# Experts in plain fp32 on column tiles of the array, with a longer ring of weights

## What is computed

```python
def swiglu(h, w_gu, w_down):
    gt, up = jnp.split(h @ w_gu, 2, axis=-1)
    return (jax.nn.silu(gt) * up) @ w_down

def moe(h, w_r, b_r, w_gu, w_down):
    t = h.reshape(-1, shp[-1])
    logits = (t @ w_r).astype(jnp.float32) + b_r.astype(jnp.float32)
    top_v, top_i = lax.top_k(logits, TOP_K)
    wts = jax.nn.softmax(top_v, axis=-1)
    comb = jnp.sum(jax.nn.one_hot(top_i, N_EXPERTS) * wts[..., None], axis=1)
    out = jnp.zeros_like(t)
    for e in range(N_EXPERTS):
        out = out + comb[:, e:e + 1] * swiglu(t, w_gu[e], w_down[e])
```

## Time and profile before

| | |
|---|---|
| median of three runs | 1997.94 us (1997.94 to 1998.37) |
| span of the profiled execution | 1993.6 us |
| PE busy | 1947.5 us, 98% |
| DVE busy | 1556.5 us, 78% |
| ACT busy | 1135.9 us, 57% |
| DMA | 523.97 MB, 262 GB/s read and written over the span |
| mean granted TensorE clock | 0.987 |

### The profile page before, as it was taken

The page is one execution under the profiler, slowest core; times in us unless marked ns, Lnnn a source line. Parts: engine busy times, 40 slices in busy tenths (PEclk is TensorE's granted clock), DMA queues, the critical chain, the costliest instruction groups (busy, mean ns, idle before and its releaser), DMA issues.

```text
span 1993.6 us, 31431 instructions
## 1 busy us (share of the span) xinstructions
PE 1947.5 (98%) x11926; PEld 1657.1 (83%) x11926; DVE 1556.5 (78%) x2210; ACT 1135.9 (57%) x1385; POOL 240.4 (12%) x279
## 2 busy tenths in 40 slices
PE   7999999999999999999999999999999999999997
PEld 3778999899998788999788888888888888888886
DVE  6895448655673976377898989989889899898996
ACT  2214334545432233334677777777778777787774
POOL 2540432000005331340000000000000000000000
PEclk9999999999999999999999999999999999999999
DMA  9575444555551564435599999999999999899993
GB/s 348 183 289 202 147 149 176 200 181 185 176 175 64 201 218 138 169 108 198 187 362 365 353 338 339 360 365 351 343 330 364 368 350 343 330 361 369 342 357 126
DMA packets 143054, 523.97 MB, mean 263 GB/s; under 512 B 16192, under 2 KB 16704, under 8 KB 142272
## 3 DMA queue, kind: packets, MB, share of 16 engines
q1 hardware_dynamic: 140544, 508.82, 70.3%
q10 hardware_dynamic: 1728, 7.90, 1.2%
q0 software_dynamic: 640, 5.35, 0.7%
HBM read 515.57 MB, written 6.43 MB: 262 GB/s over the span
## 4 chain that ended last, share of the span: by engine, by line
PE 87%; DVE 7%; ACT 2%; POOL 2%; issue 1%; DMA 1%; ACTq 0%; DVEq 0%
PE bank L1041 28%; PE bank L1066 14%; PE bank L878 12%; PE bank L291 9%; PE bank L616 8%; PE bank L479 4%; DVE wlo L2414 3%; PE bank L495 2%; PE bank L966 2%; PE bank L1028 1%; ACT whi L1408 1%; PE bank L444 1%; PE bank L837 1%; PE bank L706 1%; DMA masks<-in_masks 1%
## 5 line engine op out<-in xcount | busy, mean ns | idle before, releaser
L2414 DVE TENSOR_TENSOR wlo<-ring,whi 128x1024 fp32r<-128x1024 f32 x756 | 910.0, 1221 | 145.2 <-ACT whi L1408 142.9
L1408 ACT ACTIVATE whi<-ring 128x1024 fp32r<-128x1024 f32 x756 | 799.5, 1060 | 293.9 <-PE bank L1041 146.1
L1041 PE MATMUL bank<-whi,gh 128*128 128x512 f32 x896 | 285.6, 400 | 2.1 <-DVE wlo L2414 0.9
L1041 PE MATMUL bank<-whi,gl 128*128 128x512 f32 x896 | 279.7, 393 | 0.0
L1041 PE MATMUL bank<-wlo,gh 128*128 128x512 f32 x896 | 278.9, 393 | 0.0
L291 PE MATMUL bank<-hT,ring 128*128 128x264 f32 x864 | 204.8, 397 | 5.7 <-issue 3.0
L291 PEld LDWEIGHTS bank<-hT,ring 128*128 128x128 f32 x864 | 166.1, 195 | 41.5 <-issue 11.4
L1041 PEld LDWEIGHTS bank<-wlo,gh 128*128 128x128 f32 x896 | 168.2, 188 | 39.0
L1041 PEld LDWEIGHTS bank<-whi,gl 128*128 128x128 f32 x896 | 168.1, 188 | 38.1
L1041 PEld LDWEIGHTS bank<-whi,gh 128*128 128x128 f32 x896 | 159.5, 188 | 32.3 <-DVE wlo L2414 3.2
L1066 PE MATMUL bank<-whi,eh 128*128 128x512 f32 x448 | 142.5, 399 | 0.3
(11 more groups left out here) (431 smaller groups left out, 3115.5 us busy)
## 6 DMA issues: line engine op xcount, KB each, us to landing
ring<-in_w SPq DMA_DIRECT2D x964, 512.0 KB, 5.2
out_gdns<-arena POOLq DMA_DIRECT2D x2, 2048.0 KB, 9.4
arena<-in_gdn ACTq DMA_DIRECT2D x2, 1536.0 KB, 7.1
xT<-in_x ACTq DMA_DIRECT2D x1, 1056.0 KB, 9.2
out_y<-hT SPq DMA_DIRECT2D x4, 264.0 KB, 2.1
arena<-in_gdn ACTq DMA_DIRECT2D x2, 512.0 KB, 3.8
masks<-in_masks ACTq DMA_DIRECT2D x1, 512.0 KB, 11.3
cpk<-in_cpk SPq DMA_DIRECT2D x1, 512.0 KB, 5.3
```

The source lines that it names most:

```text
L1041: ins = pe.matmul(o[half], x[:, k, mine], w[part][:, CH * half:CH * half + CH], start=k == 0 and n == 0, stop=k == KD - 1 and n == 2)
L1408: act.activation(whi[:, m % SPL, :], ring[:, r, :], ACT.Copy).then_inc(sem("hi_done"), 1)
L2414: v.tensor_tensor(wlo[:, m % SPL, :], ring[:, (low.base + m) % RING, :], whi[:, m % SPL, :].bitcast(F32), ALU.subtract).then_inc(sem("lo_d ...
```

## The change

Tokens and weights change places in the experts, and the split goes.

- The weights of an expert are now the stationary operand, in blocks of 128 x 128 like those of the other parts of the kernel (`_slots`, `_pairs`, `_blocks` in the layout). Each block is loaded in four tiles of 32 columns (`product`, `CT`), each with its own quarter of the output partitions, and `CAP` = 96 columns of tokens stream. The products are plain fp32, so there is no split of weights, tokens or hidden values: `high` and `low` are not called for experts, `gl`, `eh`, `el` and DVE's `gathered` are gone, `gh` becomes `gx` and the hidden values `ea`.
- Results come out features by tokens. Hidden values need no transposes. The down result does: ACT copies pairs of feature tiles to `ys`, and `turn` transposes them into banks 4 and 5, where `rows` reads them.
- The ring has twelve places for experts (`ERING`): the seven of `ring`, and five in `ring2` over the former split buffers. PE waits for the landing itself (`place_sem`), and `e_used`, counted by PE, frees a place for SP. The first twelve slots are loaded without a wait for PE.
- Silu and product go over four feature tiles at once (`BAT`). `ROWS`, `COMBINE` and `DCT` move by a slot. Two pairs of input loads share a semaphore. POOL clears `yh` and `yl` too, since `rows` now writes 96 of their 128 partitions.

The diff, cut to what the steps below speak of:

```diff
-CAP = 128
+CAP = 96
...
-NCH = FF // CH
+BAT = 4
+NCH = FT // BAT
+ERING = 12
+CT = P // 32
...
-        gh, gl = over("gh", [P, KD, PAIR], where(hT), 0), over("gl", [P, KD, PAIR], arena_at, 0)
-        eh, el = over("eh", [P, FT, CAP], arena_at, 2 * B1), over("el", [P, FT, CAP], arena_at, 2 * B1 + FT * CAP)
-        at_e = 2 * B1 + 2 * FT * CAP
-        erow = ar(at_e, 2, CH)
-        srow = ar(at_e + 2 * CH, 2, CH)
+        gx = over("gx", [P, KD, PAIR], where(hT), 0, F32)
+        ea = ar(2 * B1, FT, CAP)
+        at_e = 2 * B1 + FT * CAP
+        srow = ar(at_e, 2, BAT, CAP)
+        ys = ar(at_e + 2 * BAT * CAP, KD, CAP)
+        ring2 = over("ring2", [P, ERING - RING, SLOT * P], where(whi), 0, F32)
...
-        def silu_after(m):
-
-            return [c for c in range(NCH) if m == KD * (c + 1) + SPL - 1]
-
-        def turned_after(m):
-            return [c for c in range(NCH) if m == KD * (c + 1) + TURN + SPL]
+        def batch_after(m):
+
+            return [c for c in range(NCH) if m == 2 * BAT * (c + 1)]
+
+        def half_down_after(m):
+
+            return [p for p in range(KD // YP) if m == UP_S + FT * YP // SLOT * (p + 1)]
+
+        def place(m):
+
+            p = m % ERING
+            return ring[:, (MIX1_END + p) % RING, :] if p < RING else ring2[:, p - RING, :]
+
+        def place_sem(m):
+            p = m % ERING
+            return landed[(MIX1_END + p) % RING] if p < RING else landed2[p - RING]
+
+        def place_count(q, m):
+
+            p = m % ERING
...
+                def turn(self, q, p):
+
+                    pe.wait_ge(sem("e_ys"), q * (KD // YP) + p + 1)
+                    for m in range(YP * p, YP * p + YP):
+                        ins = pe.transpose(bank[4 + m // 4][0:CAP, P * (m % 4):P * (m % 4) + P], ys[:, m, :], ident)
+                    if YP * (p + 1) % 4 == 0:
+                        ins.then_inc(sem("ye_full"), 1)
...
+                def emptied(c):
+                    if a is not None or q or c >= 2:
+                        pe.wait_ge(sem("act_done"), q * NCH + (FT + 1 + max(c - 1, 0)))
+
+                def product(out, w, b, x, first, last):
+                    for j in range(CT):
+                        ins = pe.matmul(out[32 * j:32 * j + 32, :], w[:, b * P + 32 * j:b * P + 32 * j + 32], x,
+                                        start=first, stop=last)
+                    return ins
+
                 if sub == 0:
-                    pe.wait_ge(sem("gh_done"), pg * 4 + 4)
-                    pe.wait_ge(sem("gl_done"), pg * 4 + 4)
...
-                    c, k = s // KD, s % KD
-                    pe.wait_ge(sem("lo_done"), q * FFN_S + (base + s + 1))
-                    if k == 0 and c >= 2:
-                        pe.wait_ge(sem("act_done"), q * NCH + (FT + 1 + c - 1))
-                    w = [t[:, s % SPL, :] for t in (whi, wlo)]
-                    o = [bank[2 * (c % 2) + half][0:CAP, :] for half in range(2)]
-                    for n, (x, part) in enumerate(((gh, 0), (gh, 1), (gl, 0))):
-                        for half in range(2):
-                            ins = pe.matmul(o[half], x[:, k, mine], w[part][:, CH * half:CH * half + CH],
-                                            start=k == 0 and n == 0, stop=k == KD - 1 and n == 2)
-                            if n == 0 and half == 0:
-                                ins.then_inc(sem("spl_used"), 1)
-                    if k == KD - 1:
-                        ins.then_inc(sem("up_full"), 1)
-                    if k == TURN and c:
-                        turn(c - 1)
+                    f, half = s // 2, s % 2
+                    c = f // BAT
+                    pe.wait_ge(place_sem(s), place_count(q, s))
+                    if s % (2 * BAT) == 0:
+                        emptied(c)
+                    o = bank[2 * (c % 2) + half][:, CAP * (f % BAT):CAP * (f % BAT) + CAP]
+                    for k in range(KD):
+                        ins = product(o, place(s), k, gx[:, k, mine], k == 0, k == KD - 1)
+                    ins.then_inc(sem("e_used"), 1)
+                    if a is None and s == BACK and not (q == 0):
+                        self.turn(q - 1, KD // YP - 1)
                     if s in COMBINE:
                         self.combine(s - COMBINE[0], g)
...
-                for s in range(DOWN_S):
-                    m = UP_S + s
-                    pe.wait_ge(sem("lo_done"), q * FFN_S + (base + m + 1))
-                    if s % (CH // P) == 0:
-                        pe.wait_ge(sem("turned_done"), q * NCH + (s // (CH // P) + 1))
-                    w = [t[:, m % SPL, :] for t in (whi, wlo)]
-                    for n, (x, part) in enumerate(((eh, 0), (eh, 1), (el, 0))):
-                        for half in range(2):
-                            ins = pe.matmul(bank[6 + half][0:CAP, :], x[:, s, :], w[part][:, CH * half:CH * half + CH],
-                                            start=s == 0 and n == 0, stop=s == FT - 1 and n == 2)
-                            if n == 0 and half == 0:
-                                ins.then_inc(sem("spl_used"), 1)
-                            if s == FT - 1 and n == 2:
-                                ins.then_inc(sem("ye_full"), 1)
-                    if s == TURN:
-                        turn(NCH - 1)
-                    if sub and UP_S + s in GATHER:
-                        self.gather(GATHER.index(UP_S + s), pg + 1)
+                for m in range(KD):
+                    if m % YP == 0 and (a is not None or q or m > YP):
+                        pe.wait_ge(sem("e_ys"), q * (KD // YP) + (m // YP - 1))
+                    for k in range(FT):
+                        b = m * FT + k
+                        s, i = UP_S + b // SLOT, b % SLOT
+                        if i == 0:
+                            pe.wait_ge(place_sem(s), place_count(q, s))
+                        if m == 0 and k % BAT == 0:
+                            pe.wait_ge(sem("act_done"), q * NCH + (FT + 1 + k // BAT + 1))
+                        ins = product(bank[6 + m // YP % 2][:, CAP * (m % YP):CAP * (m % YP) + CAP], place(s), i, ea[:, k, :],
+                                      k == 0, k == FT - 1)
+                        if i == SLOT - 1:
+                            ins.then_inc(sem("e_used"), 1)
+                            for p in half_down_after(s - BACK):
+                                if p == 0:
+                                    pe.wait_ge(sem("dcT_done"), q * 1 + 1)
+                                self.turn(q, p)
+                            if sub and s in GATHER:
+                                self.gather(GATHER.index(s), pg + 1)
+                if a is not None:
+                    self.turn(q, KD // YP - 1)
...
-                    sp.wait_ge(sem("lo_done"), q * FFN_S + (FFN_S + s - RING + 1))
-                    r = (MIX1_END + s) % RING
-                    sp.dma_start(ring[:, r, :], w_in[e * FFN_S + (MIX1_END + s)]).then_inc(landed[r], 16)
+                    if not (s0 and s < ERING):
+                        sp.wait_ge(sem("e_used"), q * FFN_S + (s - ERING + 1))
+                    sp.dma_start(place(s), w_in[e * FFN_S + (MIX1_END + s)]).then_inc(place_sem(s), 16)
...
-                if k >= KD - LAG:
-                    s = k - (KD - LAG)
-                    n = MIX1_END + s
-                    high(n % RING, 16 * (n // RING + 1), s, FFN_S + s + 1)
...
+                for m in range(FFN_S + 1):
+                    for c in batch_after(m):
+                        act.wait_ge(sem("e_used"), q * FFN_S + m)
+                        if not (a is None and q == 0 and c < 2):
+                            act.wait_ge(sem("act_done"), q * NCH + (FT + 1 + c - 1))
+                        act.activation(srow[:, c % 2, :, :], four(bank[2 * (c % 2)]), ACT.Silu).then_inc(sem("silu_done"), 1)
+                    for p in half_down_after(m):
+                        act.wait_ge(sem("e_used"), q * FFN_S + m)
+                        act.activation(ys[:, YP * p:YP * p + YP, :],
+                                       bank[6 + p % 2][:, 0:YP * CAP].rearrange("p (a b) -> p a b", b=CAP), ACT.Copy).then_inc(sem("e_ys"), 1)
                     if m == ROWS:
...
-                    if l and m >= KD - LAG:
-                        low(m - (KD - LAG), FFN_S + m - (KD - LAG) + 1)
...
-                    if not (a is None and e == 0 and m < LAG):
-                        low(m, q * FFN_S + (FFN_S + m + 1))
-                    for c in silu_after(m):
+                    for c in batch_after(m):
                         v.wait_ge(sem("silu_done"), q * NCH + (FT + c + 1))
-                        v.tensor_tensor(erow[0:CAP, c % 2, :], srow[0:CAP, c % 2, :], bank[2 * (c % 2) + 1][0:CAP, :],
+                        v.tensor_tensor(ea[:, BAT * c:BAT * c + BAT, :], srow[:, c % 2, :, :], four(bank[2 * (c % 2) + 1]),
                                         ALU.mult).then_inc(sem("act_done"), 1)
```

(44 more changed lines are left out.)

90 lines of the change are left out of this document (35 added, 55 removed).

## The result

The changed kernel takes 2458.4 us (median of 4 runs) beside 1998.2 us for the kernel before: a ratio of 1.228, 95% interval 1.225 to 1.231. It is slower by 23%, where 1991 us was forecast. The span of the profiled execution is 2458.3 us.

The account below looks back on a forecast made before the run. PE paced the kernel before, DMA close behind; after, one DMA engine: 1.276 us data plus 0.24 code, 1.516 a slot over 659 slots from 963.7 to 1962.7. Span 1987.0, median 1991 us, 0.3% faster; range 1840 to 2055.

Parts of the forecast that it names:

- The reading of the kernel before: Expert stage: PE sets the pace at 1.50 us a slot, DMA is near its limit, ACT and DVE splits are hidden.
- PE's cost of a slot: Experts: 32 products of 21.7 ns, 0.69 us; PE's whole work falls from 1.50 to some 0.81 us a slot.
- The price of the code: Expert stage: PE's instruction packets, one every four slots at 0.95 us, add 0.24 us a slot on one DMA engine.
- DMA's cost of data: Expert weights: 524288 bytes a slot at the full-queue rate of 411 GB/s, 1.276 us; dearer bounds 1.372 and 1.421.
- rival 2: Expert weights arrive at the expert stage's slower rate: 1.612 to 1.661 us a slot, 2054 to 2087 us; chance 0.17.
- What moves around it: Before and beside the experts: root 2.7 us sooner, last token copy 0.45 for 0.60 us, first product at 959.7 for 962.54.
- The last residual: Norm before the experts: without DVE's subtraction at 926.70 it starts about 1.1 us sooner.
- the root's input: Norm before the experts: starts about 2.7 us sooner without DVE's subtractions; 0 if the root finds another wait.
- Rival 1: Expert stage: instructions cost nothing on the path, 1.291 us a slot, 1843 us; chance 0.27.
- Rival 3: Expert stage: PE's clock falls to 1.2 GHz while waiting, about 1.62 us a slot, 2060 us at most; 0.06 with others.
- the signs named: Expert windows, if right: PE waits for landings, SP for PE, about 230 q8 packets, near 345 GB/s, landing near 18 us.

Follow-up runs that it names:

- the two-tile kernel: The changed kernel with two weight tiles of 64 columns for each 128-column block in place of four of 32: 1996.9 us, ratio 0.9996 to the kernel before.
- the fastest: The two-tile kernel with its combine and gather steps issued in pairs: 1987.8 us, ratio 0.994 to the kernel before.
- the loops: The changed kernel plus extra fp32 products in hardware loops at PE's program end; 64 calls 8 times, 256 and 512 calls 4 times: 23.1, 45.6, 128.3 us.

## Why the prediction was wrong

**The reading of the kernel before** held: PE set its pace, and ACT's and DVE's splits lay hidden.

**PE's cost of a slot is the step that failed.** The duration was right: 21.7 ns a product by interpolation, 20.5 measured. The count was not. The 64 products of line 461 in the earlier trace rows are records; the code has 32 calls there for each layer (2 halves x 2 x 2 x 4). A plain fp32 call is two loads and two products in the records. So 32 calls a slot are 64 products, 1.31 us in place of 0.69, and 128 instructions in place of 64. The row that would have told it, x64 beside 32 calls, stood in the prediction's own evidence.

**The price of the code was read rightly and put in the wrong place.** 16.4 KB a packet, about 256 instructions, about 1 us on the queue: all as measured (1.09 us on average). But the forecast charged that microsecond to a DMA engine and asked what it does to the weights. What matters is the way from one block to the next as PE sees it: 1.1 to 1.7 us until the packet starts, 1.0 for the packet, 1.4 until PE goes on. PE has its products to cover that and nothing else. At 2.63 us of products to 3.7 us of way, it can't. The term was 0.24 us a slot; the stand is 2.19 - 1.31 = 0.88 with the other products.

The two errors belong together. With 64 instructions a slot, as counted, the code would have come at 64/256 x 4.28 = 1.07 us a slot, below the 1.28 of the weights, and by this reckoning the stand would have cost next to nothing (the two-tile kernel has 64 instructions a slot, and 37 us of code stands). The doubled count makes it 2.14, which decides. The corrected sum: 964.3 (first product) + 672 x 2.19 = 2436 us; the last products of line 1053 end at 2433.6, and the kernel 25 us later (23 in the kernel before).

**DMA's cost of data** (1.276 us a slot, 411 GB/s) was not tested, since no run here let the weights set the pace: the fastest brought 356 GB/s with PE busy for 97%. It stays open, and with it rival 2.

**What moves around it** was small, as said, and came out in sum but not in its parts. The forecast had the first product 2.8 us sooner. Counted from the start of the mixer's last product (926.34 before, 931.35 after), it comes after 33.0 us in place of 36.2, and after 32.9 to 33.5 in the other runs with this code. The last residual starts 1.2 us sooner by that count, as read (1.1), but the root's input (931.62 before) 1.3 us sooner and not 2.7. It finds another wait, as the low bound of that term allowed, for PE's products of the norm:

```profile
931.35 0.28 PE L641 MATMUL bank<-ml,ghi 128*128 128x264 f32 x1
931.67 0.17 DVE L2216 TENSOR_TENSOR tmp<-bank,mods 128x8 f32<-128x8 f32 x1 [1.99 <-PE bank L641]
935.30 0.43 DVE L1559 TENSOR_SCALAR tmp<-bank 128x264 f32<-128x264 f32 x1 [2.54 <-PE bank L428]
```

The other 1.9 us lie between there and the first product, where 0.15 was forecast. In that stretch the granted clock was first 0.50, the level of 1.2 GHz, for 6.8 us in place of 10.2, and the router's 48 products took 6.59 us in place of 7.51; why is open. That the sum came out was luck. (The first product came at 964.32 and not 959.7, since the mixer ended later; its last product started between 924.6 and 934.3 us in the runs with this code.)

**The rivals.** None gave the time. Rival 1, code that costs nothing, is the opposite of what happened. The Trainium skill, "Runtime: NRT & Kernel Launch", Instruction fetch mechanics, calls the crossing of a 16 KiB block mostly hidden; the trace agrees on the block (a stand every 256 instructions) and not on the hiding (363.5 us of stands from 1000 to 2400 us). The same section of the Trainium skill gives TensorE room for 2048 instructions; the loops don't contradict it, with a body of 1024 that stayed and one of 2048, beside the loop's own instructions, that was fetched anew. Rival 3 is out with a granted clock of 0.96. Of the signs named, the one that was decisive did its work: q8 packets were to be about 230 and are 395, and PE was to wait for landings and does not.

## What to carry to other kernels

Count instructions in the records, not calls in the source, before a price is put on them, and hold the time that 256 of them keep the engine against the time until the next code is there: here 3.7 to 4.4 us, so products of 20 ns written out run at 0.6 to 0.7 of their speed, while the same products in a loop of up to 1024 instructions run at full. Halving the calls with tiles of 64 columns, which cost the same for a block, took back the whole loss. Keep products of one tile size together: a change between 32 and 64 columns costs about 0.14 us.

## What the runs showed of the hardware

- A plain fp32 call is recorded as two loads and two products; a 128x128 block against 96 columns costs 2 x 111.9 = 224 ns in one tile, 4 x 41.5 = 166 in two and 8 x 20.5 = 164 in four.
- Where a block of 256 instructions runs for less time than this, the code of the next comes 3.74 us after that of the last with the DMA queues idle, and 4.28 us beside 246 GB/s of weights; with blocks cut to three quarters of their time or made a third longer it was 4.00 and 4.39 us.
- Code that stays from one turn of a loop to the next (1024 instructions did, 2048 did not) is not waited for.
- A change between tiles of 32 and 64 weight columns makes TensorE stand for 0.144 us; the page counts that as busy.
